# A hybrid decoder step on one core: six inner iterations written out in place of a loop on the engines

## The reference, cut to what matters

```python
proj = rmsnorm(x, norm_mix_g) @ w_in
ya, wkv_new, shift_new = rwkv_group(proj[..., :P_A], ...)     # 8 heads of 64, a delta state carried over time
yc, v_rows = chunk_mlp(proj[..., P_A:], ...)                  # gated MLP within chunks of 128 tokens
x = x + jnp.concatenate([ya, yc], axis=-1) @ w_out
x = x + peer_ffn(rmsnorm(x, norm_ffn_g), ...)                 # 8 heads x 16 experts of 16384 for each token
gate = sigmoid(rmsnorm(x, norm_ple_g) @ ple_gate_w)
x = x + (p @ ple_w) * gate
y = rmsnorm(x, norm_final_g)
```

## Time and profile before

| | |
|---|---|
| median of 3 runs | 4069.53 us (4062.77 to 4085.47) |
| profiled execution | 4059.65 us |
| its span, first to last instruction | 4057.9 us |
| granted TensorE clock, mean | 0.89 |
| busy share of the span | PE 74%, DVE 74%, POOL 59%, PEld 42%, ACT 21% |
| moved by DMA | 1399.82 MB, mean 345 GB/s |

### The profile page before, as it was taken

The page is one execution under the profiler, slowest core; times in us unless marked ns, Lnnn a source line. Parts: engine busy times, 40 slices in busy tenths (PEclk is TensorE's granted clock), DMA queues, the critical chain, the costliest instruction groups (busy, mean ns, idle before and its releaser), DMA issues.

```text
span 4057.9 us, 42806 instructions
## 1 busy us (share of the span) xinstructions
PE 3001.7 (74%) x11794; PEld 1710.7 (42%) x11794; DVE 3009.5 (74%) x6485; ACT 866.6 (21%) x1753; POOL 2408.2 (59%) x2129
## 2 busy tenths in 40 slices
PE   6757788778776787778776787778776777753776
PEld 3743455336542455335532455336532455211431
DVE  2458876789569886789578876789579976788582
ACT  1111211322121311321121312221121212220112
POOL 1017775677556774577556774677556774575541
PEclk8778889989999899989999899989899899986778
DMA  5069999999999999999999999999999999998975
GB/s 163 31 222 389 348 362 384 398 375 354 376 347 416 349 370 373 374 372 359 374 360 416 347 372 360 385 369 363 365 354 416 341 377 369 372 351 307 357 273 209
DMA packets 453893, 1399.82 MB, mean 345 GB/s; under 512 B 44129, under 2 KB 55681, under 8 KB 453650
## 3 DMA queue, kind: packets, MB, share of 16 engines
q0 software_dynamic: 297216, 1082.26, 69.6%
q1 hardware_dynamic: 156434, 314.66, 21.0%
HBM read 1386.84 MB, written 9.93 MB: 344 GB/s over the span
## 4 chain that ended last, share of the span: by engine, by line
DVE 32%; PE 31%; DMA 16%; issue 12%; ACT 5%; PEld 2%; POOL 1%; DVEq 0%; SPq 0%; ACTq 0%; PEldq 0%; POOLq 0%
PE peer_acc L1038 10%; DVE uring L1737 7%; DMA wbuf<-in_peer_wq_dram 5%; PE bank L795 4%; DMA wbuf<-in_w_in_dram 4%; DVE accv L1730 4%; DMA wbuf<-in_w_out_dram 3%; PE bank L900 2%; PE bank L953 2%; DMA vring<-in_peer_v_dram,eidx 2%; PE bank L951 2%; PEld bank L900 1%; PE bank L955 1%; PE bank L756 1%; PE bank L1015 1%
## 5 line engine op out<-in xcount | busy, mean ns | idle before, releaser
L700 POOL DMA_INDIRECT uring<-in_peer_u_dram,eidx x1024 | 1193.2, 1165 | 947.1 <-issue 532.9
L712 POOL DMA_INDIRECT vring<-in_peer_v_dram,eidx x1024 | 1183.9, 1156 | 606.1 <-PE peer_acc L1038 306.3
L1038 PE MATMUL peer_acc<-vring,dg 128*128 128x512 f32 x2368 | 1229.2, 664 | 375.6 <-ACT dg L1086 340.2
L1737 DVE CUSTOM_DVE_ANT_0 uring<-uring,px 128x1024 f32<-128x1024 f32 x1024 | 1239.9, 1222 | 52.5 <-DMA uring<-in_peer_u_dram,eidx 21.1
L1038 PEld LDWEIGHTS peer_acc<-vring,dg 128*128 128x128 f32 x2368 | 473.8, 211 | 964.1 <-issue 641.1
L795 PE MATMUL bank<-wbuf,xT 128*128 128x512 f32 (+3 forms) x1440 | 665.1, 606 | 195.3 <-DMA wbuf<-in_w_in_dram 117.9
L1730 DVE SCALAR_TENSOR_TENSOR accv<-vring,pact,accv 128x1024 f32<-128x1024 f32 x424 | 545.2, 1286 | 71.9 <-DMA vring<-in_peer_v_dram,eidx 44.3
L795 PEld LDWEIGHTS bank<-wbuf,xT 128*128 128x128 f32 (+1 forms) x1440 | 262.9, 191 | 591.1 <-issue 279.0
L900 PE MATMUL bank<-xT,wbuf 128*128 128x128 f32 (+1 forms) x2304 | 299.8, 289 | 60.7 <-DMA wbuf<-in_peer_wq_dram 58.1
L900 PEld LDWEIGHTS bank<-xT,wbuf 128*128 128x128 f32 x2304 | 292.3, 208 | 85.0 <-DMA wbuf<-in_peer_wq_dram 68.9
L1086 ACT ACTIVATE dg<-ident,pact 128x128 f32<-128x128 f32 x592 | 200.4, 392 | 507.3 <-DVE pact L1718 498.7
(11 more groups left out here) (296 smaller groups left out, 3229.6 us busy)
## 6 DMA issues: line engine op xcount, KB each, us to landing
wbuf<-in_w_in_dram SPq DMA_DIRECT2D x198, 512.0 KB, 10.8
wbuf<-in_peer_wq_dram SPq DMA_DIRECT2D x144, 512.0 KB, 9.6
wbuf<-in_w_out_dram SPq DMA_DIRECT2D x72, 512.0 KB, 10.5
wbuf<-in_ple_gate_w_dram SPq DMA_DIRECT2D x72, 512.0 KB, 7.0
uring<-in_peer_u_dram,eidx POOLq DMA_INDIRECT x1024, 7.5
vring<-in_peer_v_dram,eidx POOLq DMA_INDIRECT x1024, 7.6
wbuf<-in_ple_w_dram SPq DMA_DIRECT2D x18, 512.0 KB, 12.3
ms<-in_shift_mu_dram SPq DMA_DIRECT2D x9, 896.0 KB, 12.0
```

Source lines behind the costliest of these rows:

```text
L700: gp.indirect_dma_start(uring[:, s, :], None, peer_u, expert_rows(n, j)).then_inc(sig(f"u{s}_full"), 16)
L712: gp.indirect_dma_start(vring[:, s, :], None, peer_v, expert_rows(n, j)).then_inc(sig(f"v{s}_full"), 16)
L1038: last = mm(acc[c][:, :], dg[:, n % 2, at, :], vring[:, s, c * 512:(c + 1) * 512], start=(n + at == 0), stop=(n == UNITS - 1 and j == pe_e ...
L1737: v.tensor_tensor_reduce(out=uring[:, s, :], in0=uring[:, s, :], in1=px[:, :], scale=1.0, scalar=0.0, op0=ALU.mult, op1=ALU.add, accum_out ...
```

## The change

The loop over iterations 2 to 7 on every engine becomes a Python loop, so that each engine's program holds these six iterations one after the other, with i a number. What an iteration computes, and the order of its stages, stays.

```diff
             iteration(0, False, False)
             iteration(1, False, True)
-            with eng.Fori(2, NB) as i:
+            for i in range(2, NB):
                 iteration(i, True, True)
             iteration(NB, True, True)
             handoff(NB + 1)
```

## The result

The changed kernel takes 4033.2 us (median of 6 runs, 4021.95 to 4045.4), the kernel before 4067.49 (6 runs, 4053.51 to 4085.47). The ratio is 0.9916 with an interval of 0.989 to 0.9942: 34 us less, 24 to 45 by the interval. The forecast was 17.9 us less. The time lies in the range, the direction is the forecast's, and the size is twice it.

What follows compares the result with a forecast made beforehand. VectorE, TensorE and transfers were all taken as near their limit, ruling by stage. 20.4 + 3.5 = 23.9 us, less a quarter 17.9, took 4059.65 to 4041.7; 9.9 for the median gave 4052 us, range 4020 to 4078.

Steps and rivals of the forecast that it cites:

- The branch, 3.5 us: At the loop's boundary: removing five taken branches wins 0.70 us each, 3.5 us in all.
- The cover argument: At the loop's boundary: TensorE's 15.98 us run of 32 expert products hides the branch stops, VectorE's being some 4.4 us.
- 8.8 us were foretold for L1683: VectorE's wait for TensorE behind the loop's boundary: near 8.8 us in all iterations once no branch is taken.
- The 0.70 us that came through: From the search's last step (L1558) to the load of x (L512): mean of differences 0.93 and 0.47 us per branch.
- The register instructions, 20.4 us: In six iterations: 34 exposed register instructions each, at 0.10 us, give 3.4 us an iteration, 20.4 us in all.
- the count of exposed ones: In iteration 4's chain: of 53 register instructions 19 are hidden and 34 stand in a real pause.
- A quarter off for the streaming stage: Stage streaming `w_in`, about 100 of 454 us, is paced by transfers, so 23.9 us of gain becomes 17.9.
- That transfers hold it: Rival, chance 0.20: DMA engines, busy 0.97 of each inner iteration, are the limit; time stays within 8 us of 4069.
- That all was on the path: Rival, chance 0.20: branch stops and all register instructions count fully, 66 us off, giving 4003; half of it gives 4036.
- The slower one: Rival, chance 0.10: straight code is read too late, stopping engines 4.4 us each; one stop per iteration gives 4078.
- the sign that the prediction named: Inside an iteration: pauses of 4 us without a releaser would show the prediction wrong.
- the bound of 447 us: Windows of inner iterations, foretold at about 451 us: below 447 would mean more was exposed than counted.

Runs made afterwards that it cites:

- e4_two: Kernel before, loop and register instructions kept, two iterations written into one turn, so two taken branches in place of five: 4074.72 us, ratio 1.0011.
- e5_hint: Kernel before, loop and all five taken branches kept, each branch announced to the instruction fetch: 4071.66 us, ratio 1.0021 against the kernel before.
- e9_again: The change once more, unaltered, measured against the kernel before on the same chip: 4026.08 us, ratio 0.9901.
- three single runs: Kernel before with six iterations written out only on VectorE (4060.71 us), only on TensorE (4051.52), or only on ScalarE, GpSimd and SyncE (4059.05).
- Dosed kernels: The change plus one idle register instruction ahead of waits in iterations 2 to 7: on TensorE 4053.38 us, on VectorE 4050.04, on all five engines 4062.30.
- e11_no_settle_pe: The change without the semaphore increment that TensorE issues after a stage (`settle`): 4023.73 us, ratio 0.9886 against the kernel before.

## Why the prediction was right in direction and half in size

**The branch, 3.5 us: nothing was won.** The cover argument held: TensorE's 32 products hide both stops. But the stop turned into two waits where the prediction named one. On average of iterations 3 to 7, L1683 waits 7.7 us in place of 5.7, and 2.6 us are waits for gathered rows, where there were none. 8.8 us were foretold for L1683 in every iteration; they are 8.53, 8.51, 5.66, 8.39, 7.31 and 8.66 in iterations 3 to 8. L1661 follows after 0.03 us, not 0.3. VectorE's branch row of 68 ns is also shorter than the 108 ns set beside it. The 0.70 us that came through were read from three distances, 34.11, 33.65 and 33.18 us. Before, the five distances with a taken branch are 33.62 to 34.11 us, 33.82 on average; after the change the same distance, without any branch, is 32.81 to 34.65 us in iterations 3 to 8, 33.80 on average. So the difference was spread and no price. e4_two and e5_hint, which change the branch alone, gain nothing, and from L1558 to L1392, where the branch lies, the mean is unchanged. The Trainium skill, Runtime: NRT & Kernel Launch, section Instruction fetch mechanics, says that a taken branch out of the window stalls; here it does, and the stall isn't on the path.

**The register instructions, 20.4 us: the right cause, with TensorE's share nearly left out.** The step that failed is the count of exposed ones from named pieces of the chain. On TensorE such a register instruction mostly has no piece of its own; it lengthens the "issue" behind the releaser, at L953 from 0.14 to 0.23 us. So the count found 2 on TensorE among 34. In iteration 4 of before, 16 of the 51 pauses of TensorE in the trace end with such an instruction, which makes 6 x 16 x 0.09 = 9 us, an estimate that takes each pause in full; 2.9 of them are at L953. In iteration 4 of the change no pause has one. TensorE's loop on its own was worth 15 us, 7 to 24, where the count gave 6 x 2 x 0.10 = 1.2. For VectorE, 12 us of the sum by 20 pieces, its loop alone gave 4.5 us (-4 to 13), which doesn't exclude 12. The price of 0.10 us for each was close to the measured 0.09. Where L1737 follows L1415 the 0.14 us are gone, as foretold; timeline of DVE, iteration 3:

```profile
1332.65 0.69 DVE L1415 TENSOR_TENSOR z<-uv,ft 128x512 f32<-128x512 f32 x1
1333.38 1.23 DVE L1737 CUSTOM_DVE_ANT_0 uring<-uring,px 128x1024 f32<-128x1024 f32 x1
```

**A quarter off for the streaming stage: right in its direction.** There nothing was won that can be told (174.89 us, then 174.82 and 173.98). But the gain of the rest was 4.2 us for an iteration, not three quarters of 3.4. The six iterations gave 25.5 and 31.2 us in the two profiled executions of the change, 17.9 were forecast.

**The rivals.** That transfers hold it fell: the windows of iterations 4 and 6 went to 447.7 and 451.7 us at a DMA share of 0.98. That all was on the path gave 4036 for its half, the nearest figure of all, but not by its reason: the 22 us of branch it contains were worth nothing. The slower one, late reads of straight code, does not show: q8 has fewer packets, and VectorE has no pause put down to issue of more than 1.1 us other than at L1730, and TensorE none over 1.0. At L1730 the longest is 4.2 us, which by its length is the sign that the prediction named; but both kernels wait for gathered rows there, and its pauses are 71.9 us in all before and 73.8 after. The shortest iteration came near the bound of 447 us (447.70), and in e9_again two fell below it (446.19 and 446.75, from one L1661 to the next), which was to say that more was exposed than I counted.

**What stays open.** The three single runs sum to 25 us against 34 and 40 for the whole; each has an interval of some 8 us to either side, so that a surplus of the combination is neither shown nor excluded. Dosed kernels don't add up either: 20 to 27 and 18 to 24 us for one engine, 31 to 37 for all. How much of the rest is ScalarE's, GpSimd's or SyncE's was not taken apart, and so the 396 `settle` instructions that left SyncE have no price of their own. Nor is it shown how a shorter pause turns into time: at L953 writing out TensorE's loop took 2.9 us of pauses away and e11_no_settle_pe 7.3 us more, and only the first came with a gain that can be told. And both profiled executions of the change are one sample each, set against one of the kernel before.

## What to carry to other kernels

A loop on the engines costs what its counts cost: where engines hand short work to each other, a wait that ends just ahead of such a register instruction is 0.09 us longer. Here 110 of them for an iteration on TensorE, 16 of them exposed in the one iteration counted, went with some 15 us over six iterations (7 to 24), while the branch, whose stop is nearly 5 us, lay under other work and cost nothing that can be told. Count such instructions from the pauses of every engine (pause with and without one, by the same line), not from the pieces of the chain, which can hide them in "issue"; and check the sum by a run, since a shorter pause need not show in the time (e11_no_settle_pe). And before you price a small difference between two iterations, look at how much the same distance varies in all of them.

## What the runs showed of the hardware that was not expected

- Behind a taken branch VectorE pauses for 4.1 to 4.7 us; on TensorE the branch stands for 5.6 us. With the hint to the instruction fetch this falls to 1.0 and 0.35 us (e5_hint).
- A register instruction (ALU_OP) takes 32 to 41 ns by its row. Behind a release it lengthens the pause by 0.09 us. Spread over all waits it cost little: 6 x 398 = 2388 more on TensorE, with 551 semaphore instructions fewer, cost 20 to 27 us. That is some 10 ns for each added one, or 11 to 15 ns if the 551 are taken off; measured against 0.09 us, an estimate, five in six to nine in ten are hidden.
- A semaphore instruction of 51 ns costs TensorE as much behind a release: without it the pause falls from 0.14 to 0.04 us, 0.09 on average over 80 (e11_no_settle_pe).
- Code that is the same in both kernels runs differently by when the TensorE clock is granted. Windows of the stretch 66 to 80 us, in iteration 0 (columns as in the earlier trace rows), before:

```profile
66.00:80.00 14.00, 14.00 (x26) 5.65 (x25) 4.53 (x5) 0.60 (x1) 0.00 (x0) 0.68 0.06 21
```

and after:

```profile
66.00:80.00 14.00, 12.35 (x36) 5.66 (x34) 5.62 (x8) 2.09 (x4) 0.00 (x0) 1.00 0.11 40
```

The mean granted clock is 0.68 and 1.00 (the upper level, 2.4 GHz), and in the same 14 us the second gets through 36 products against 26. In e9_again, which has the program of the change, it is as before (0.67, 25 products). So such a difference between two single executions is no effect of the change. The kernel before alone ran from 4043 to 4091 us over its executions, so medians of several runs are needed for a difference of this size.
